# Taking the three products of a split weight by kind instead of by output inside each K-tile

## What is computed

```python
z = h @ w_in                                  # attention, 2048 -> 5120 columns
u, gate = jnp.split(h @ w_in, 2, axis=-1)     # Fourier mixer, 2048 -> 8192
proj = jnp.einsum("bsd,dp->bsp", n, w_in)     # second block, 2048 -> 13344
jnp.einsum("bsf,fd->bsd", jax.nn.silu(gate) * val, w_ffn_out)
```

## Time and profile before

| | |
|---|---|
| median of three executions | 3289.17 us |
| the profiled execution: its own time | 3289.61 us |
| its span, first to last instruction | 3287.8 us |
| mean granted TensorE clock | 0.967 of 2.4 GHz |
| PE busy, and weight loads busy | 3130.6 and 2880.1 us |
| DVE, ACT, POOL busy | 1855.7, 1268.5, 246.5 us |
| matmuls, and weight loads | 23262 and 23262 |
| mean rate of the transfers | 167 GB/s |

### The profile page before, as it was taken

One profiled execution on the slowest core, in us unless ns is written; L12 is line 12 of the kernel. 1 busy time (PEld: TensorE's weight loads), 2 busy tenths in 40 slices (PEclk: granted clock), 3 DMA queues, 4 the chain that ended last, 5 costly groups with the idle time before them and its releaser, 6 DMA issues.

```text
span 3287.8 us, 52600 instructions
## 1 busy us (share of the span) xinstructions
PE 3130.6 (95%) x23262; PEld 2880.1 (88%) x23262; DVE 1855.7 (56%) x2132; ACT 1268.5 (39%) x1326; POOL 246.5 (7%) x244
## 2 busy tenths in 40 slices
PE   6999999988999999999999999998989999999998
PEld 3699775588989998989999989977979999999998
DVE  6736755476756434464554537755445666456653
ACT  7623331235433333343333325432233444344443
POOL 0001001000000000002211200032300000000000
PEclk8999999998999999989999989989989999999999
DMA  8746545363655554434444425500024555555553
GB/s 339 296 174 228 207 148 179 115 227 137 249 213 210 180 179 151 144 135 168 150 164 155 154 103 186 186 14 1 1 97 160 181 191 183 188 186 188 187 182 132
DMA packets 90850, 548.04 MB, mean 167 GB/s; under 512 B 10592, under 2 KB 10624, under 8 KB 45568
## 3 DMA queue, kind: packets, MB, share of 16 engines
q1 hardware_dynamic: 69408, 465.86, 39.9%
q0 software_dynamic: 18432, 67.12, 5.7%
q10 hardware_dynamic: 2784, 11.70, 0.9%
HBM read 542.54 MB, written 2.10 MB: 166 GB/s over the span
## 4 chain that ended last, share of the span: by engine, by line
PE 88%; DVE 6%; ACT 2%; issue 2%; DMA 1%; SPq 0%; DVEq 0%; ACTq 0%
PE bank L663 87%; DVE r L1812 2%; ACT r L1242 1%; DMA f<-in_units 1%; PE bank L725 1%; DVE f L1846 0%; PE bank L994 0%; DVE f L1865 0%; DVE f L2351 0%; ACT f L1359 0%; DVE f L2121 0%; DMA f<-in_later 0%; DVE f L2240 0%; DVE f L1988 0%; DVE f L2138 0%
## 5 line engine op out<-in xcount | busy, mean ns | idle before, releaser
L663 PE MATMUL bank<-r,r 128*128 128x256 f32 (+4 forms) x19360 | 2468.3, 288 | 62.6 <-DVE r L1812 33.7
L663 PEld LDWEIGHTS bank<-r,r 128*128 128x128 f32 (+3 forms) x19360 | 2355.0, 188 | 167.7 <-issue 75.7
L1812 DVE TENSOR_TENSOR r<-f,r 128x2048 fp32r<-128x2048 f32 (+2 forms) x466 | 1012.8, 2176 | 907.9 <-ACT r L1242 907.7
L1242 ACT CAST r<-f 128x2048 fp32r<-128x2048 f32 (+2 forms) x466 | 834.9, 1794 | 1036.0 <-PE bank L663 889.5
L663 PE MATMUL bank<-f,f 128*128 128x128 f32 (+12 forms) x3390 | 639.5, 338 | 51.1 <-issue 7.3
L663 PEld LDWEIGHTS bank<-f,f 128*128 128x128 f32 (+6 forms) x3390 | 472.9, 196 | 163.5 <-issue 88.3
L1846 DVE SCALAR_TENSOR_TENSOR f<-f,f,f 128x512 f32<-128x512 f32 x240 | 180.0, 750 | 42.6 <-DMA f<-in_later 35.5
L2540 POOL DMA_DIRECT2D f<-in_later x128 | 67.8, 529 | 980.1 <-DVE f L1846 801.6
L1259 ACT COPY f<-bank 128x512 f32<-128x512 f32 (+2 forms) x141 | 80.0, 587 | 158.4 <-PE bank L663 152.5
L2289 DVE SCALAR_TENSOR_TENSOR f<-f,f,f 128x255 f32<-128x255 f32 (+1 forms) x272 | 131.7, 484 | 9.7
L2549 POOL TENSOR_TENSOR f<-f,f 32x512 f32<-32x512 f32 x24 | 31.0, 1292 | 745.9 <-PE bank L663 745.9
(11 more groups left out here) (205 smaller groups left out, 879.9 us busy)
## 6 DMA issues: line engine op xcount, KB each, us to landing
f<-in_units SPq DMA_DIRECT2D x346, 1024.0 KB, 4.8
f<-in_units SPq DMA_DIRECT2D x120, 768.0 KB, 4.3
f<-in_later POOLq DMA_DIRECT2D x128, 512.0 KB, 4.9
f<-in_units SPq DMA_DIRECT2D x8, 576.0 KB, 4.6
f<-in_x ACTq DMA_DIRECT2D x2, 1024.0 KB, 12.8
f<-in_ctx ACTq DMA_DIRECT2D x2, 1024.0 KB, 11.3
f<-in_x_turned ACTq DMA_DIRECT2D x1, 2048.0 KB, 11.5
f<-in_units SPq DMA_DIRECT2D x2, 800.0 KB, 4.4
```

The source lines that it names most:

```text
L663: return e.matmul(o, lhsT, rhs, start=start, stop=stop, skip_group_check=True)
L1242: e.copy(unit_view(high[HIGH_OF[u]][1], u), unit_view(raw[RAW_OF[u]][0], u)).then_inc(*up("w_hi", ("hi", u)))
L1812: e.tensor_tensor(unit_view(raw[RAW_OF[u]][1], u), unit_view(raw[RAW_OF[u]][0], u), unit_view(high[HIGH_OF[u]][1], u).bitcast(F32), ALU.su ...
```

## The change

Inside a K-tile the loop over the kinds moves outside the loop over the pieces: first the high by high matmuls of all pieces, then the high by low ones, then the low by high ones. In the last unit of the four `ENDS` layers, which goes by output, the kinds go outside the K-tiles of that output. The `first` flag goes to the first matmul of kind 0 alone, and the `last` one to the last kind. The claims stay ahead of the first matmul to a bank, which is now the third matmul of the layer for the second bank and the fifth for the third. The semaphore increments stay on the last matmul of a bank and on the last of a unit.

```diff
--- before.py
+++ after.py
@@ -668,33 +668,33 @@
             u, k0, k1 = L.us[n], L.cuts[n], L.cuts[n + 1]
             e.wait_ge(*at("lo", u) if L.split else at("landed", u))
             sets = [(q, x) for q, members in enumerate(L.groups) for x in range(len(members))]
-            steps = [(kt, q, x) for kt in range(k0, k1) for q, x in sets]
+            kinds = range(3 if L.split else 1)
+            steps = [(kt, kind, q, x) for kt in range(k0, k1) for kind in kinds for q, x in sets]
             by_output = n == L.n - 1 and name in ENDS
             if by_output:
                 for kt in range(k0, k1):
                     for step in (ready(kt) if ready is not None else []):
                         e.wait_ge(*at(*step))
-                steps = [(kt, q, x) for q, x in sets for kt in range(k0, k1)]
-            for kt, q, x in steps:
+                steps = [(kt, kind, q, x) for q, x in sets for kind in kinds for kt in range(k0, k1)]
+            for kt, kind, q, x in steps:
                 i, m, off, cols = L.groups[q][x]
-                if not by_output and q + x == 0:
+                if not by_output and kind + q + x == 0:
                     for step in (ready(kt) if ready is not None else []):
                         e.wait_ge(*at(*step))
-                if kt == 0 and x == 0:
+                if kt == 0 and kind == 0 and x == 0:
                     held[q] = claim(e, LINS, "lin", name, q)
                 o = held[q][0:m, off:off + cols]
-                first, last = kt == 0 and x == 0, kt == L.kts - 1
+                first = kt == 0 and kind == 0 and x == 0
+                last = kt == L.kts - 1 and kind == kinds[-1]
                 if L.split:
-                    hi = unit_cut(high[HIGH_OF[u]][1], u)[:, kt - k0, :]
-                    lo = unit_cut(raw[RAW_OF[u]][1], u)[:, kt - k0, :]
-                    mm(e, o, *operands(kt, i, hi, 0), first, False)
-                    mm(e, o, *operands(kt, i, hi, 1), False, False)
-                    ins = mm(e, o, *operands(kt, i, lo, 0), False, last)
+
+                    buf = (raw[RAW_OF[u]] if kind == 2 else high[HIGH_OF[u]])[1]
+                    ins = mm(e, o, *operands(kt, i, unit_cut(buf, u)[:, kt - k0, :], kind % 2), first, last)
                 else:
                     w = unit_cut(raw[RAW_OF[u]][0], u)[:, kt - k0, :]
                     ins = mm(e, o, *operands(kt, i, w), first, last)
                 names = [("ps", "lin", name, q)] if last and x == len(L.groups[q]) - 1 else []
-                if (kt, q, x) == steps[-1]:
+                if (kt, kind, q, x) == steps[-1]:
                     names.append(("used", u))
                 if names:
                     ins.then_inc(*up("pe_linear", *names))
```

## The result

The changed kernel takes 3293.21 us, the median of twelve executions (3287.29 to 3297.92), against 3287.08 for the kernel before in the same rounds (also twelve, 3281.00 to 3292.64). The ratio is 1.0019, with a 95% interval from 1.0011 to 1.0028: 6.1 us slower by the medians, where 5.9 were forecast. As a time 3295.1 was forecast, from the 3289.17 of the first three executions; it lies 1.9 us too high because the kernel before takes 2.1 us less here.

The account below looks back on a forecast made before the run. PE was taken as the bound: 19360 L663 matmuls times their pace, plus PE's waits. Terms 2.6 + 2.2 + 0.5 + 0.2 + 0.2 + 0.2 = 5.9 us gave a median of 3295.1 us, range 3289.0 to 3301.0.

Parts of the forecast that it names:

- The sign of being wrong: Prediction wrong if ff's long piece doesn't move from 2518.36 to about 2524, or its length changes by more than 1 us.
- Part 1, the pace: All L663 matmuls: the new order costs 0 ns per product, at 117.8 ns from start to start.
- ckv: Start of ckv: earlier claim of qb0's bank waits for ACT's copy and prolongs the slow clock; 2.6 us, bounds 1.1 and 4.1.
- dv at hf 1 to 3: dv's fifth matmul waits 0.73 us for ACT's copy of dk's bank, three places; 2.2 us, bounds 1.5 and 3.
- The other dilated layers: Eight other dilated layers: 0.1 us each from dq to dk at hf 1 to 3, little elsewhere; 0.5 us, bounds 0 and 1.5.
- kpe: kpe waits for ACT's second copy of ckv's banks, now complete closer together; 0.2 us, bounds 0 and 0.4.
- The head: cq's second and third banks, claimed sooner, wait some 0.2 us each, part absorbed; 0.2 us, bounds 0 and 0.5.
- The ends of layers: ACT's last copy of a layer ends 0.24 us later, which counts only at z's two silus; 0.2 us.
- Absorbed waits: Rival: PE's later start finds work ready that it waits for today; 3289.2 to 3291 us, chance 0.21.
- The clock falling at dv: Rival: new waits at ckv and dv at hf 1 to 3 lower PE's clock; 12 us slower, 3301, chance 0.15.
- The quick state: Rival: more matmuls run at 112.3 to 113 ns; 26 us gained in the last long stretch, 3269, chance 0.06.

Follow-up runs that it names:

- the control: The kernel before, unchanged, compared against itself; ratio 1.0009 (1.0000 to 1.0018).
- e7: The changed kernel with six extra products of 32 by 256 ahead of the first product at twelve layers; 3271.73 us, ratio 0.9974 to the kernel before.
- e11: The changed kernel with six extra products of 32 by 256 at 17 layers, eight of them in ff; 3282.07 us, ratio 0.9992.
- e4: The changed kernel with ACT's copies of qb0's two banks moved ahead of the cast; ratio 1.0015 to the kernel before.
- `first`: The kernel before with the order by kind in the first K-tile of each layer alone; one execution, 3297.12 us.
- e9: The kernel of e1 measured a second time against the kernel before; ratio 1.0003 (0.9984 to 1.0022).
- e1: The changed kernel with the first and last K-tile of every layer by output again; ratio 1.0012 (0.9998 to 1.0026) to the kernel before.
- `middle`: The order of e1 and e9, by kind only between a layer's first and last K-tile; ratios 1.0012 and 1.0003 to the kernel before.
- e6: The kernel before with six extra products of 32 by 256 ahead of the first product at twelve layers; 3255.09 us, ratio 0.9922.
- e10: The kernel before with six extra products of 32 by 256 at 17 layers, eight of them in ff; 3262.95 us, ratio 0.9933.

## Why the prediction was right

*The sum.* 5.9 us were forecast. The places that follow the order add up to 6.3 in the traces: ckv 2.28, kpe 0.89, dv 3 x (0.62 + 0.32) = 2.82, dq at hf 2 and 3 2 x 0.17 = 0.34. The agreement with the measured 6.1 us is closer than either deserves: the control lies 0.0009 from 1, so the measured difference could as well be 3 or 9 us. The places are the firmer number, and in them too there was luck: kpe and dv cost more than their terms, the other terms less.

*The sign of being wrong.* I had written that the prediction is wrong if the start of ff's long piece in the chain doesn't move from 2518.36 to about 2524. In the changed kernel's trace it doesn't:

```profile
2517.53 682.97 PE bank L663 x5776
```

By that sign the waits would be absorbed. But the sign can't tell: the same piece starts at 2511.52 in the control, the same program, and anywhere from 2507.55 to 2525.82 in the traces of the other orders, so the places of the last two rows of the table outweigh 6 us. It is the medians of twelve executions, with an interval that begins at 1.0011, that show the loss. The other half of the sign holds, as the length is 682.97 in both the earlier trace rows.

*Part 1, the pace.* Right for the 256-column products of the long layers. From ff 1 to oX 1 0, 5088 products, both orders take 599.25 us to the hundredth. Neither the bank that changes every second product, nor the lost repetition of a stationary tile costs anything there. The granted clock is 1.00 from 2600 to 2700 in the changed kernel, in e7 and in e11, all with the order by kind. The Trainium skill's rule in "TensorE: Matmul & The Clock Gate", section "A second HAM failure mode: psum-queue depth-cycling", by which a kernel that cycles through PSUM banks makes PE idle for moments and can lose its clock by that, has no case in this stream. The quick pace is 113.3 ns and not 112.3: five of the 136 records that I counted for it were short products of other forms.

*ckv.* 2.6 forecast, 2.28 measured, and by the mechanism named: the wait of 1.49 us, then one more slow stretch. e4 removed it by moving two copies on ACT.

*dv at hf 1 to 3.* The fifth product was to be 0.73 us late. By the starts it is 0.64 late, and the first unit is 0.62 longer: its next two steps lose 0.1 us, and 0.14 come back, since PE leaves the wait at 113 ns a product where it ran at 118 before. A second part was not forecast: the next six units run 0.32 us longer each time. After the side steps three of them now fall into the slow pace where they had the quick one (0.14 to 0.16 us each), and one the other way. `first`, which has the same wait and otherwise the old order, shows the same 30.06. In e7 PE leaves the wait at 118 ns, the first unit takes 6.25 us, and the next six take 29.74 as before; so this part hangs on the state that PE is in, not on the order as such.

*The other dilated layers.* 0.5 forecast, 0.34 measured, at dq and not at dk where I had looked for it: dk's first units at hf 1 lose 0.17 and its others win 0.16. This is the least firm of the terms. Taken whole, the dq and dk layers and the first dv are 1.1 us longer in the changed kernel's trace, but they are 1.0 longer in e9 and 0.3 shorter in e1, whose claims stand as before. Steps of 0.15 to 0.17 us, the two paces again, come and go in them.

*kpe.* 0.2 forecast, 0.89 measured over the whole layer. The sentence that the 64-column pieces show no price was wrong: the term was mis-sized because they have one. By the starts of the products, in the old order six 64-column ones in a row at 118 ns are followed by twelve 128-column ones, most of them at 113 to 114, and a K-tile takes 2.08 us. Taken two by two, four 128-column ones follow at 113 to 123, and it takes 2.12. `middle`, with the claims where they were, loses 0.55 of the 0.89 in this way, in its 14 K-tiles; the first K-tile with its early claim takes 2.37 in place of 2.07.

*The head.* cq's first unit is 0.45 us longer, near the 0.4 of two waits, and ckv begins no later than before (185.52 against 185.70). Nothing of it is seen there, where I had counted 0.2; but this start lies between 184.98 and 186.77 in the traces of all orders, so a loss of 0.2 could not be seen either.

*The ends of layers.* 0.2 forecast. Not to be seen: the stretch from z to oM takes any value from 278.4 to 284.0 us in any order.

*The rivals.* Absorbed waits: the median says no, and a trace can show it only place by place, as said above. The clock falling at dv: no. The window of 1449 to 1930 stood at 0.99 before and reads 1.00 in the changed kernel's profile, and dv's units lengthen by the wait and the state alone. The quick state: it exists, it lasts, and it is worth much more than the whole change, but nothing shows that the change brings it. For all 19360 products it would be worth 19360 x 4.5 ns = 87 us, not the 80 I wrote. I gave it as a state that PE falls into after some interruptions. That fits: executions of the kernel before at 3265.0, 3267.4, 3265.8 and 3252.8 are on record beside a median of 3284, and so is one of e9 at 3256.2. That one was profiled; ff ran at the quick pace in it with no extra product anywhere:

```profile
2600.00:2700.00 100.00, 100.00 (x885) 100.00 (x884) 70.53 (x86) 46.66 (x38) 0.00 (x0) 1.00 0.56 191
```

In e1's profiled execution, 3278.48 us, the layers from qkv 1 to z 1 ran at 113.3 ns in the same way. For the four others this is an inference from their times alone.

## What to carry to other kernels

When the order of equal products changes inside an accumulation, the products cost the same (where wide and narrow ones mix, as in kpe, they may not); look at the two ends, where banks are claimed and where they are complete, count the products between the two for each bank, and hold that against the copy and against what stands ahead of the copy in its engine's queue. A change of a few microseconds in three thousand is read from the distances between named instructions in two traces, and with a control, since one comparison of times can be a thousandth off. Where a margin is lost because a copy stands behind other work, moving the copy is the cheap mend.

## What the runs showed of the hardware

A steady stream of float32r products with 256 moving columns has at least two paces at full clock, 117.8 and 113.3 ns, and keeps the one it has for thousands of products. Side work, waits and small products can change it. Six products of 32 stationary columns, 0.7 us, brought or kept the quick one in ff and qkv in the traces of e6, e7 and e10 and failed in ff in that of e11, and the best kernel here is the one before with those at twelve layers: 3255.09 us, 0.78% below it. The slow pace seems to have more than one form, as equal tries failed eight times in a row where unequal ones left a single heap of times. What in TensorE makes the paces was not found; the weight load's record is 188 ns long in the slow pace and in the quick one (e6, 2600 to 2700), and products with 512 moving columns stayed at 233 ns in every trace.
